# Issuing the first attention head's keys and queries ahead of the second gate unit's weights, and splitting those weights later

## The reference

```
u = RMSNorm(h)
[xp | q | k | v | gate_logits] = u @ w_in
y_pool = (causal pooling mixer on xp) @ w_branch_pool
y_sb   = (stick-breaking attention on q, k, v; 8 heads of 64) @ w_branch_attn
m = sigmoid(g_pool) * y_pool + sigmoid(g_sb) * y_sb
h = h + m @ w_out
```

## Time and profile before

| | us |
|---|---|
| median of 3 runs | 1917.36 |
| lowest and highest | 1917.35, 1918.03 |
| profiled execution, whole | 1918.11 |
| its span, first to last instruction | 1916.2 |
| PE busy in the span | 1903.5 |
| DVE, ACT, POOL busy | 1372.2, 796.4, 115.9 |

### The profile page before, as it was taken

The page is one execution under the profiler, slowest core; times in us unless marked ns, Lnnn a source line. Parts: engine busy times, 40 slices in busy tenths (PEclk is TensorE's granted clock), DMA queues, the critical chain, the costliest instruction groups (busy, mean ns, idle before and its releaser), DMA issues.

```text
span 1916.2 us, 24977 instructions
## 1 busy us (share of the span) xinstructions
PE 1903.5 (99%) x9010; PEld 1592.0 (83%) x9010; DVE 1372.2 (72%) x1677; ACT 796.4 (42%) x1175; POOL 115.9 (6%) x157
## 2 busy tenths in 40 slices
PE   9999999999999999999999999999999999999998
PEld 8888888888888888888888888898888888888887
DVE  6978777784566776488677768889777777756555
ACT  7423232323434544234676752474323232324344
POOL 1000000000000300000233220010000000000001
PEclk9999999999999999999999999999999999999999
DMA  5456654558676733416875447643545444677665
GB/s 165 144 198 230 223 181 140 199 189 306 208 240 201 195 110 132 132 50 181 226 174 148 128 139 260 197 138 119 178 144 196 149 169 153 216 264 244 206 192 206
DMA packets 258419, 348.24 MB, mean 182 GB/s; under 512 B 29344, under 2 KB 161184, under 8 KB 255008
## 3 DMA queue, kind: packets, MB, share of 16 engines
q1 hardware_dynamic: 258336, 347.15, 56.3%
HBM read 233.83 MB, written 112.99 MB: 181 GB/s over the span
## 4 chain that ended last, share of the span: by engine, by line
PE 97%; DVE 1%; DMA 1%; issue 0%; SPq 0%; ACT 0%; POOL 0%; POOLq 0%; DVEq 0%; ACTq 0%
PE bank L1263 40%; PE bank L1372 9%; PE bank L1319 9%; PE bank L1321 9%; PE bank L1320 9%; PE bank L1513 6%; PE bank L1215 3%; PE bank L1449 2%; PE bank L1421 2%; PE bank L1479 2%; PE bank L1585 2%; PE bank L1604 1%; PE bank L1190 1%; PE bank L1603 1%; PE bank L1570 1%; PE bank L1568 1%
## 5 line engine op out<-in xcount | busy, mean ns | idle before, releaser
L2253 DVE TENSOR_TENSOR dn_lo<-dn_lo_raw,dn_hi 128x1024 fp32r<-128x1024 f32 x149 | 181.9, 1224 | 149.6 <-ACT dn_hi L1788 149.1
L1263 PE MATMUL bank<-lo_t,wa_hi 128*128 128x512 f32 x656 | 252.8, 389 | 0.0
L1263 PE MATMUL bank<-hi_t,wa_hi 128*128 128x512 f32 x656 | 252.8, 389 | 0.0
L1263 PE MATMUL bank<-hi_t,wa_lo 128*128 128x512 f32 x656 | 252.8, 389 | 0.0
L1788 ACT ACTIVATE dn_hi<-dn_lo_raw 128x1024 fp32r<-128x1024 f32 x149 | 158.0, 1061 | 218.8 <-DMA dn_lo_raw<-act_dram 218.8
L1319 PE MATMUL bank<-dn_hi 128*128 128x512 f32 x596 | 232.7, 390 | 0.0
L1321 PE MATMUL bank<-dn_lo,dn_hi 128*128 128x512 f32 x596 | 231.9, 389 | 0.0
L1320 PE MATMUL bank<-dn_hi,dn_lo 128*128 128x512 f32 x596 | 231.9, 389 | 0.0
L1263 PE MATMUL bank<-hi_b,wa_hi 128*128 128x512 f32 x492 | 190.6, 389 | 1.0 <-DVE up L2387 1.0
L1263 PE MATMUL bank<-lo_b,wa_hi 128*128 128x512 f32 x492 | 190.5, 389 | 0.0
L1263 PE MATMUL bank<-hi_b,wa_lo 128*128 128x512 f32 x492 | 190.4, 389 | 0.0
(11 more groups left out here) (275 smaller groups left out, 3747.7 us busy)
## 6 DMA issues: line engine op xcount, KB each, us to landing
wa_lo_raw<-in_ffn_w_gate_up_dram SPq DMA_DIRECT2D x87, 512.0 KB, 5.0
dn_lo_raw<-act_dram SPq DMA_DIRECT2D x149, 256.0 KB, 4.2
act_dram<-g SPq DMA_DIRECT2D x44, 512.0 KB, 4.4
wd_t<-in_ffn_w_down_dram SPq DMA_DIRECT2D x44, 512.0 KB, 6.6
act_dram<-s_of SPq DMA_DIRECT2D x88, 256.0 KB, 6.5
wd_dram<-wd_t SPq DMA_DIRECT2D x22, 1024.0 KB, 6.0
dn_lo_raw<-wd_dram SPq DMA_DIRECT2D x85, 256.0 KB, 3.4
dn_lo_raw<-in_ffn_w_down_dram SPq DMA_DIRECT2D x64, 256.0 KB, 3.0
```

Source lines behind the costliest of these rows:

```text
L1263: last = nc.tensor.matmul(acc, lhs, rhs, start=n == 0 and i != 2 and i < 5, stop=n == 11, skip_group_check=True)
L2253: return nc.vector.tensor_tensor(dst, raw, hi.bitcast(f32), ALU.subtract)
```

## The change

```diff
 def piece_step(j, piece):
 
-    return gate_step(piece_start(j) + (7 + 18 * piece if j < NG - 1 else 1 + 6 * piece))
+    return gate_step(piece_start(j) + (20 if j == 1 else 7) + 18 * piece if j < NG - 1 else piece_start(j) + 1 + 6 * piece)
...
             gate_unit(0)
             spill_pool_branch(2)
-            gate_unit(1)
...
             load_head(0)
+            gate_unit(1)
             spill_pool_branch(3)
             load_head(1)
```

## The result

The changed kernel takes 1922.41 us (median of 10 runs, 1921.78 to 1923.74) against 1917.62 before (10 runs beside it): a ratio of 1.0024, with a 95% interval of 1.0015 to 1.0034. It is 4.8 us slower. The forecast was 1918.7, within 1916.0 to 1919.9, so the time lies above the range. The profiled execution took 1921.93, with a span of 1920.1, somewhat less than its kernel's median.

A forecast was written before the change was run, and what follows sets the result against it. PE, busy 1903.5 of 1916.2 us, was taken as the bound. The 1.2 us gain at the keys is swallowed by a 2.4 us stall at tile 2's turn: net +1.3 on 1917.36 gives 1918.7, range 1916.0 to 1919.9.

The forecast's parts named there:

- when the read-back lands: Pooling sums' read-back on SP's queue: 3.0 us later, from 924.6 to 927.6, with bounds of 2.0 to 3.6 later.
- the gain at the keys: PE's 1.77 us wait on head 0's last key load: PE goes on 0.5 to 1.77 us earlier, taken as 1.2.
- The landing of the weights: Moved gate weights, issued from 911.7 on behind head 0's loads: the second DMA lands at 918.2.
- The drain of the four stores: Pooling stores behind the weights in the DMA queue: 2.5 us, done at 920.7, which is 3.2 later than before.
- the slack: At tile 2's turn on PE: before, 927.2 was possible while PE came only at 928.95, so 1.75 us.
- The way from landing to PE: From the read-back through POOL's product and mask and DVE's scan to PE's turn of tile 2: 2.6 us.
- The further 0.3: Tile 2's scan on DVE could wait for POOL's second mask, 0.29 us more, making the net +1.5.
- the net at the turn: Tile 2's turn on PE moves from 928.95 to 930.2, +1.25 us, after PE stands idle for 2.4 us.
- The pieces: Four ACT and four DVE pieces of the weights, split 13 products later: number unchanged, cost nothing.
- The 1.0 us to spare: ACT's wait for the pooling stores ahead of tile 2's sigmoids: met at 920.7, against 921.7.
- Slower by over 0.2%: Rival, chance 0.05: the read-back is pushed much further, its queue shifted by 7.2 us, +5.45 us, so 1922.8.
- Keys only: Rival, chance 0.25: the read-back lands within the slack, PE keeps part of the 1.2 us, 1915.6 to 1917.0.

The follow-up runs named there:

- e2: The kernel before with only the gate weights' pieces split 13 products later, DMA order as before: 1917.73 us against 1917.83.
- e7: The kernel before with the third gate unit's weights, 1 MB, issued ahead of the two read-backs instead of behind them: 1922.30 us against 1917.53.
- e9: The kernel before with only POOL's products of gate banks 0 and 1 done two steps later: 1917.62 us against 1917.53.
- e8: The changed kernel with 12 unused matmuls put into PE's queue just ahead of tile 2's turn: 1920.56 us against 1917.53 for the kernel before.
- e1: The kernel before with only the second gate unit's weights issued behind head 0's loads, pieces split where they were: 1922.65 us against 1917.83.
- e3: The changed kernel with POOL's products of gate banks 0 and 1 two steps later, behind the masks: 1916.81 us against 1917.83 for the kernel before.
- e10: The kernel of e6 with the second pair's values loaded in step 5 instead of step 2: 1916.86 us against 1917.69 for the kernel before.
- e4: The changed kernel with the first of the two weight DMAs back ahead of the keys: 1919.30 us against 1917.83 for the kernel before.
- e6: The changed kernel with last pooling stores and read-backs ahead of the weights, pieces at products 44, 54, 64, 74: 1917.70 us against 1917.53 for the kernel before.

## Why the prediction was wrong

The mechanism was the forecast's; its size was not. Two terms failed, each for about half of the miss: when the read-back lands, and what the clock loses behind PE's stall.

- *What bounds the kernel, and the gain at the keys.* Right in kind. The loads of the keys kept their issue times, the last landed after 3.50 us where 3.0 to 4.0 were bounds, and the wait shrank as said. From 912.03 + 0.23 to 913.00 (PE's last matmul before the wait starts at 912.03) are 0.74 us, so 1.77 - 0.74 = 1.03 us was won in this pair of traces; 1.2 was taken. The wait of 1.6 us before was a long one: with the same order of loads it is 1.2, 1.1 and 1.2 in e2, e7 and e9, by which only 0.5 to 0.6 was won. The estimate of 2.3 us that the prediction worked out from the formula of the Trainium skill, SBUF — State Buffer, section "The DMA setup-cost knee", is not borne out by this load, which took 3.50; the first of the twelve took 2.8.
- *The landing of the weights.* Nearly right: 918.3, or 918.6 with the 0.33 between the traces, taken as 918.2.
- *The drain of the four stores.* Longer than taken, but this alone didn't make the read-back late. It was taken as 2.5 us in all, so 920.7. ACT's first sigmoid of tile 2, which waits for them, starts at 921.95 after a wait of 0.37, so they were done only near 921.9, or 922.2 with the 0.33. But head 1's first load landed at 916.78 + 5.0 = 921.8, no later than they did. And in e8 the stores were done at 921.6 and SP issued the read-back right then, at 921.66, yet it landed at 929.2 all the same.
- *When the read-back lands, and the slack.* This step failed. The forecast was 924.6 + 3.0 = 927.6; it landed at 928.9 + 0.33 = 929.2. The 924.6 came from a single trace. In e2 and e9 SP's queue is the same up to the read-back, and there it landed later. These rows answer to the earlier trace rows, first e2, then e9:

```profile
918.70 0.93 SPq L1016 DMA_DIRECT2D pool_y<-g_dram  x2
pool_y<-g_dram SPq DMA_DIRECT2D x1, 256.0 KB, 7.7
...
918.68 1.24 SPq L1016 DMA_DIRECT2D pool_y<-g_dram  x2
pool_y<-g_dram SPq DMA_DIRECT2D x1, 256.0 KB, 7.2
```

Laid side by side at the first key load, the three landings of the old order are 924.6, 926.5 and 925.8, in the mean 925.6. With both weight DMAs moved they are 929.2 (the changed kernel), 929.0 (e1), 929.8 (e3) and 929.2 (e8), in the mean 929.3. So the push was 3.7 us, where 3.0 was taken and 3.6 was the upper bound, and the value that it was added to was 1.0 too early. The slack of 1.75 us was that of the one trace; in e2, 926.5 + 2.6 = 929.1 leaves none, as the turn comes at 928.94. Why landings of the same load lie up to 1.9 us apart isn't known. SP, too, came later to the read-back than was taken: the stores held its queue for 4.03 us in place of 2.25, and it was issued at 921.93 + 0.33 = 922.3, not near 920.8. In e8 it was issued 0.6 earlier and landed no earlier, so the issue alone doesn't explain it; what does stays open.

- *The way from landing to PE.* Right: 931.32 - 928.9 = 2.4 us, taken as 2.6. The further 0.3 weighed for tile 2's scan did not come: it took 0.70, and 0.68 before. PE's wait was forecast as 2.4 and is 3.7, and the net at the turn was forecast as 1.25 and is 2.7, by the late landing. With this error alone the time would have been about 1920.3, just above the range.
- *What a wait costs.* The missing term, and the other half of the miss. The sum counted a stall of PE as its length. No sentence asked what PE's clock does behind it. In e8 this was worth 1.8 us. The kernel before shows no such stretch in the attention, as its longest wait there is 1.6 us, and its clock there is 1.00 throughout, so its rows gave no price; but a forecast that puts in a longer wait than any its trace shows should have carried a bound for it.
- *The pieces.* Right: free (e2). That they were needed is right too: left in place they made ACT wait 3.68 us (e1), though it was the read-back, not that, which set the time. The 1.0 us to spare ahead of tile 2's sigmoids was not there: ACT waited 0.37 for the stores, without effect, as tile 2's mask came later still.
- *The rivals.* "Slower by over 0.2%" had 0.05 and a price of 1922.8. Its shift of the queue of over 5.6 us did not come; half clock did the rest. That its price lies near the result is chance. "Keys only" is what e3 and e10 show once the read-back is taken out of the way, at -0.8 to -1.0 us where -1.2 was in the sum.

## What to carry to other kernels

In one DMA queue that is full, moving a transfer back doesn't remove it; follow the queue down to the first consumer without slack, and ask which in-order engine passes the wait on. Here it was POOL, where an operation without hurry stood ahead of one in a hurry, and turning those two around won back the whole loss (e3 against the changed kernel: 5.6 us), while by itself it is worth nothing (e9). Take a landing time read from one trace as one draw out of several: here three of the same order lay up to 1.9 us apart, more than the slack that was read from one of them. Count a stall of PE as its length plus what its clock may lose behind it, above all when it would be the longest of the stretch.

## What the hardware showed that was not expected

- PE stood idle for 3.66 us and then ran at a granted clock of 0.50 until about 935.4, some 3.4 us; after 3.16 us of idle time in e7 it did the same, and after 2.62 in e1's and 1.41 in e4's profiled execution it did not. The Trainium skill, TensorE: Matmul & The Clock Gate, section "Why this matters for your kernels", warns of idle gaps between bursts of matmuls, as they bring the clock down to half; the traces agree, with 0.50 behind the gaps of 3.66 and 3.16.
- Twelve matmuls of no use made the changed kernel 1.8 us faster (e8).
- The load of the second pair's values, two DMAs of 256 KB, held SP's queue for 6.9 us in e6, and with it a store that had nothing to do with it.
- The same read-back, behind the same DMAs, landed at 924.6, 926.5 and 925.8 in three traces.
